# Attention of a hybrid decoder layer: two turns of a loop over head pairs, or one list of 32 items

## The reference

```python
scale = DIFF_HEAD_DIM ** -0.5                       # 64 ** -0.5
logits = einsum('bqhcd,bkhcd->bhcqk', q_blk, k) * scale
logits = logits + bias                              # rel_bias[rel_bucket(dist)]
logits = where(dist >= 0, logits, -inf)
p = softmax(logits, axis=-1)
attn = p[:, :, 0] - lam * p[:, :, 1]                # two maps c = 0, 1 for each head
out = einsum('bhqk,bkhe->bqhe', attn, v)
out = rms_norm(out, subln_g) * (1.0 - lam_init)
```

## Time and profile before

| | |
|---|---|
| median of 3 timed runs | 2877.3 us (2871.14 to 2883.05) |
| the profiled execution | 2897.03 us |
| its span, first to last instruction | 2895.3 us |
| mean granted TensorE clock in it | 0.964 of full |
| `mix`, from its first instruction to its last | about 317 to 502 us of the span |
| its attention loop, turn one and turn two | 325.5 to 406.2, 406.2 to 487.7 us |

### The profile page before, as it was taken

The page is one execution under the profiler, slowest core; times in us unless marked ns, Lnnn a source line. Parts: engine busy times, 40 slices in busy tenths (PEclk is TensorE's granted clock), DMA queues, the critical chain, the costliest instruction groups (busy, mean ns, idle before and its releaser), DMA issues.

```text
span 2895.3 us, 42514 instructions
## 1 busy us (share of the span) xinstructions
PE 2689.3 (93%) x15119; PEld 2367.3 (82%) x15119; DVE 2324.9 (80%) x4258; ACT 1265.2 (44%) x2394; POOL 1077.8 (37%) x779
## 2 busy tenths in 40 slices
PE   7999776979998999999999999988999999999998
PEld 4888544768888999999999999986777777777777
DVE  3562477447889999999899776659999999999998
ACT  4211466222222499999898872222222222222222
POOL 0000000001114444444445665535555555555552
PEclk8999887989999999999999999999999999999999
DMA  6640000314348788989899999989999999999997
GB/s 225 235 169 12 10 0 16 130 73 136 114 133 281 270 313 302 340 301 329 285 330 336 378 379 370 367 303 369 377 389 388 385 384 388 363 387 389 383 376 260
DMA packets 310035, 794.35 MB, mean 274 GB/s; under 512 B 26592, under 2 KB 125568, under 8 KB 305792
## 3 DMA queue, kind: packets, MB, share of 16 engines
q0 software_dynamic: 110592, 402.70, 38.1%
q1 hardware_dynamic: 176832, 301.73, 29.6%
q10 hardware_dynamic: 22464, 88.09, 7.6%
HBM read 694.11 MB, written 98.30 MB: 274 GB/s over the span
## 4 chain that ended last, share of the span: by engine, by line
PE 36%; DVE 17%; DMA 12%; issue 9%; ACT 4%; SPq 1%; DVEq 0%; ACTq 0%
PE ps_up L392 29%; DVE row_sum L119 10%; DMA stage<-v_cols 8%; PE ps_g L439 4%; PE ps_y L802 3%; DMA expert_gate<-g_buf 2%; DMA stage<-expert_act 1%; DVE acc L856 1%; DVE coef_lo L877 1%; ACT key_distance L331 1%; DMA stage<-cols 1%; ACT v_hi L769 1%; DVE fetched L114 1%; ACT second_gate L335 1%; PE ps_g L407 1%
## 5 line engine op out<-in xcount | busy, mean ns | idle before, releaser
L96 POOL DMA_INDIRECT fetched<-u_rows,row_index x384 | 558.3, 1454 | 706.8 <-DVE row_act L114 588.5
L96 POOL DMA_INDIRECT fetched<-v_cols,row_index x384 | 515.4, 1342 | 423.4 <-DVE row_sum L119 367.8
L392 PE MATMUL ps_up<-h_hi,col_hi 128*128 128x320 f32 (+1 forms) x2288 | 555.1, 323 | 38.5 <-DVE col_lo L484 20.0
L392 PE MATMUL ps_up<-h_lo,col_hi 128*128 128x320 f32 (+1 forms) x2288 | 547.3, 320 | 0.0
L392 PE MATMUL ps_up<-h_hi,col_lo 128*128 128x320 f32 (+1 forms) x2288 | 546.7, 319 | 0.0
L114 DVE CUSTOM_DVE_ANT_0 fetched<-fetched,h_rows_then_gates 128x1024 f32<-128x1024 f32 x384 | 452.8, 1222 | 55.5 <-DMA fetched<-u_rows,row_index 42.3
L119 DVE SCALAR_TENSOR_TENSOR row_sum<-fetched,row_act,row_sum 128x1024 f32<-128x1024 f32 x381 | 486.8, 1278 | 1.5 <-DVE row_sum L119 0.5
L802 PE MATMUL ps_y<-v_hi,coef_hi 128*128 128x512 f32 x1280 | 406.0, 399 | 61.6 <-DVE coef_lo L877 57.1
L392 PEld LDWEIGHTS ps_up<-h_hi,col_hi 128*128 128x128 f32 x2288 | 387.8, 190 | 51.0 <-issue 35.2
L769 ACT ACTIVATE v_hi<-stage 128x1024 fp32r<-128x1024 f32 x128 | 135.9, 1062 | 647.9 <-DMA stage<-v_cols 638.1
L802 PE MATMUL ps_y<-v_lo,coef_hi 128*128 128x512 f32 x1280 | 400.6, 395 | 0.0
(11 more groups left out here) (245 smaller groups left out, 3487.3 us busy)
## 6 DMA issues: line engine op xcount, KB each, us to landing
stage<-cols SPq DMA_DIRECT2D x144, 512.0 KB
stage<-v_cols SPq DMA_DIRECT2D x128, 512.0 KB
expert_act<-stage ACTq DMA_DIRECT2D x128, 320.0 KB
expert_gate<-g_buf ACTq DMA_DIRECT2D x20, 2048.0 KB
stage<-expert_act SPq DMA_DIRECT2D x128, 320.0 KB
z_t<-w_ada SPq DMA_DIRECT2D x48, 512.0 KB, 6.1
g_raw<-expert_gate SPq DMA_DIRECT2D x64, 320.0 KB
h_rows_then_gates<-expert_gate SPq DMA_DIRECT2D x64, 320.0 KB
```

The costliest lines, as they stand in the source:

```text
L96: nc.gpsimd.indirect_dma_start(self.buf[:, n % NBUF], None, rows, bass.IndirectOffsetOnAxis(ap=self.at[:, tile, k:k + 1], axis=0)).then_in ...
L392: mm = pe.matmul(ps_up[:, b, half, 0:width], w[:, b, k], h[:, k, a:a + width], start=(k == 0 and i == 0), stop=(k == DC - 1 and i == 2))
```

## The change

The loop over pairs goes. All 32 items (4 heads x 8 query blocks) are one list `ITEMS`, in the order i = 1, 3, 5, 7, 6, 4, 2, 0, each for all four heads, and every engine's list is written out for g = 0 to 31. TensorE's and VectorE's order within an iteration is what it was. ScalarE's becomes far_part(g+2), exps(g+1), copy_t(g), squares(g-2). The scores read q and k directly from slabs 4 to 11 of `z_t`; the scaling by 64 ** -0.5 is given to the ScalarE activations of groups 4 and 5 in `in_project`. The copies at the start of a turn, `far_pair`, `pair_free`, `pair_ready` and the resets of the VectorE step counter are gone; semaphore counts and addresses are constants. Cut to its core:

```diff
@@ in_project, scalar
-                        nc.scalar.activation(z_t[:, m], ps[:, j], ACT.Gelu_apprx_tanh if p < 2 else ACT.Copy).then_inc(copied, 1)
+                        nc.scalar.activation(z_t[:, m], ps[:, j], ACT.Gelu_apprx_tanh if p < 2 else ACT.Copy,
+                                             scale=DH ** -0.5 if p in (4, 5) else 1.0).then_inc(copied, 1)
@@ mix
-        pair_qk = z_t[:, 0:4]
+        q, k = z_t[:, HEADS_A:2 * HEADS_A], z_t[:, 2 * HEADS_A:3 * HEADS_A]
         rising = list(range(1, TT, 2))
-        ORDER = [(a, i) for i in rising + [i - 1 for i in rising[::-1]] for a in range(2)]
-        FAR = [0]
-        for m in range(PAIR):
-            FAR.append(FAR[-1] + (ORDER[m][1] >= 2))
+        ITEMS = [(h, i) for i in rising + [i - 1 for i in rising[::-1]] for h in range(HEADS_A)]
+        N = len(ITEMS)
+        FAR = [sum(i >= 2 for _, i in ITEMS[:g]) for g in range(N + 1)]
@@ mix, scalar
-            with loop(nc, act, 0, HEADS_A // 2) as w:
-                act.wait_ge(pair_free, w + 1)
-                nc.scalar.activation(pair_qk[:, 2:4], z_t[:, bass.ds(8 + 2 * w, 2)], ACT.Copy).then_inc(pair_ready, 1)
-                far_part(w, 0)
-                far_part(w, 1)
-                exps(w, 0)
-                for m in range(PAIR):
-                    if m + 1 < PAIR:
-                        exps(w, m + 1)
-                    if m + 2 < PAIR:
-                        far_part(w, m + 2)
-                    copy_t(w, m)
-                    if m >= 1:
-                        squares(w, m - 1)
-                squares(w, PAIR - 1)
-                act.wait_ge(sq_sum, PAIR * w + PAIR)
+            far_part(0)
+            far_part(1)
+            exps(0)
+            for g in range(N):
+                if g + 2 < N:
+                    far_part(g + 2)
+                if g + 1 < N:
+                    exps(g + 1)
+                copy_t(g)
+                if g >= 2:
+                    squares(g - 2)
+            squares(N - 2)
+            squares(N - 1)
+            act.wait_ge(sq_sum, N)
@@ mix, tensor
-                if m == 0:
-                    pe.wait_ge(pair_ready, 3 * w + 3)
...
-                            mm = pe.matmul(at[:, c, 0:k1 - k0], pair_qk[c * DH:c * DH + DH, hh, i * P:i * P + P],
-                                           pair_qk[c * DH:c * DH + DH, 2 + hh, k0:k1], start=True, stop=True)
+                            mm = pe.matmul(at[:, c, 0:k1 - k0], q[rows, h, i * P:i * P + P], k[rows, h, k0:k1], start=True, stop=True)
...
-            with loop(nc, pe, 0, HEADS_A // 2) as w:
-                pe.wait_ge(pair_free, w + 1)
-                logits(w, 0)
-                logits(w, 1)
-                for m in range(PAIR):
+            logits(0)
+            logits(1)
+            for g in range(N):
@@ mix, vector
-            ch.reset()
-
-            dve.sem_inc(pair_free, 1)
-            with loop(nc, dve, 0, HEADS_A // 2) as w:
-
-                nc.vector.tensor_scalar(pair_qk[:, 0:2], z_t[:, bass.ds(4 + 2 * w, 2)], DH ** -0.5, None, ALU.mult).then_inc(pair_ready, 1)
-                nc.vector.tensor_copy(far_pair[:], far[:, bass.ds(2 * w, 2)]).then_inc(pair_ready, 1)
...
-                output(w, PAIR - 1)
-                dve.wait_ge(o_done, PAIR * w + PAIR)
-                dve.sem_inc(pair_free, 1)
-                ch.reset()
+            for g in range(2):
+                near(g)
+                maximum(g)
+            for g in range(N):
+                combine(g)
+                if g + 2 < N:
+                    near(g + 2)
+                    maximum(g + 2)
+                if g >= 1:
+                    output(g - 1)
+            output(N - 1)
```

More of the change, by code:

```diff
@@ L1574, in far_part @@
[L1574 to L1578, removed]
-                for c in range(2):
[L1580 to L1589, removed]
@@ new lines, in far_part @@
+                if g >= NL:
+                    act.wait_ge(comb_done, g - NL + 1)
+                bias = far[:, h:h + 1]
+                copy = nc.scalar.activation(logit[:, g % NL, :, 0:min(n, HALF)], ps_first[:, :, 0:min(n, HALF)], ACT.Identity, bias=bias)
+                if n > HALF:
+                    act.wait_ge(near_done, g + 1)
+                    copy = nc.scalar.activation(logit[:, g % NL, :, HALF:n], ps_rest[:, :, 0:n - HALF], ACT.Identity, bias=bias)
+                copy.then_inc(far_done, 1)
@@ new lines, in exps, with copy_t @@
+            def exps(g):
+                n = (ITEMS[g][1] + 1) * P
+                act.wait_ge(max_done, g + 1)
+                for c in range(2):
+                    nc.scalar.activation(logit[:, g % NL, c, 0:n], logit[:, g % NL, c, 0:n], ACT.Exp, bias=nmax[:, g % 2, c:c + 1],
+                                         accum_out=ssum[:, g % 2, c:c + 1]).then_inc(exp_done, 1)
+            def copy_t(g):
+                n = ITEMS[g][1] + 1
+                act.wait_ge(t_done, g + 1)
+                if g >= 2:
+                    act.wait_ge(o_mm, g - 1)
+                nc.scalar.activation(att_t[:, g % 2, 0:n], ps_t[:, 0:n], ACT.Copy).then_inc(t_copied, 1)
@@ L1642, in logits, with turn @@
                         if k1 == n:
                             mm.then_inc(l_done, 1)
-            def turn(w, m):
-                pe.wait_ge(comb_done, PAIR * w + m + 1)
-                if m:
-                    pe.wait_ge(t_copied, PAIR * w + m)
-                for j in range(ORDER[m][1] + 1):
-                    mm = pe.transpose(ps_t[:, j], att[:, m % 2, j * P:j * P + P], ident[:])
-                mm.then_inc(t_done, 1)
-            def values(w, m):
-                i = ORDER[m][1]
-                pe.wait_ge(t_copied, PAIR * w + m + 1)
-                if m >= 2:
-                    pe.wait_ge(o_done, PAIR * w + m - 1)
-                col = SW + (2 * w + ORDER[m][0]) * VD
+            def turn(g):
+                pe.wait_ge(comb_done, g + 1)
+                if g:
+                    pe.wait_ge(t_copied, g)
+                for j in range(ITEMS[g][1] + 1):
+                    mm = pe.transpose(ps_t[:, j], att[:, g % 2, j * P:j * P + P], ident[:])
+                mm.then_inc(t_done, 1)
@@ L1659, in values @@
+            def values(g):
+                h, i = ITEMS[g]
+                pe.wait_ge(t_copied, g + 1)
+                if g >= 2:
+                    pe.wait_ge(o_done, g - 1)
+                col = SW + h * VD
                 for j in range(i + 1):
-                    mm = pe.matmul(ps_o[:, m % 2, 0:VD], att_t[:, m % 2, j], z_n[:, j, bass.ds(col, VD)],
-                                   start=(j == 0), stop=(j == i))
+                    mm = pe.matmul(ps_o[:, g % 2, 0:VD], att_t[:, g % 2, j], z_n[:, j, col:col + VD], start=(j == 0), stop=(j == i))
@@ L1675, in _ @@
+            for g in range(N):
+                if g + 2 < N:
+                    logits(g + 2)
+                if g >= 1:
+                    values(g - 1)
+                turn(g)
+            values(N - 1)
             for t in range(TT):
@@ L1746, in _ @@
-            ch.reset()
-            dve.sem_inc(pair_free, 1)
-            with loop(nc, dve, 0, HEADS_A // 2) as w:
-                nc.vector.tensor_scalar(pair_qk[:, 0:2], z_t[:, bass.ds(4 + 2 * w, 2)], DH ** -0.5, None, ALU.mult).then_inc(pair_ready, 1)
-                nc.vector.tensor_copy(far_pair[:], far[:, bass.ds(2 * w, 2)]).then_inc(pair_ready, 1)
-                for m in range(2):
-                    near(w, m)
-                    maximum(w, m)
-                for m in range(PAIR):
-                    combine(w, m)
-                    if m + 2 < PAIR:
-                        near(w, m + 2)
-                        maximum(w, m + 2)
-                    if m >= 1:
-                        output(w, m - 1)
-                output(w, PAIR - 1)
-                dve.wait_ge(o_done, PAIR * w + PAIR)
-                dve.sem_inc(pair_free, 1)
-                ch.reset()
+                if g >= 2:
+                    dve.wait_ge(t_done, g - 1)
```

110 lines of the change are left out of this document (47 added, 63 removed).

## The result

| | before | after |
|---|---|---|
| median of the timed runs | 2876.8 us (4 runs, 2871.1 to 2883.1) | 2838.4 us (4 runs, 2832.6 to 2847.5) |
| ratio | | 0.9869 (0.9835 to 0.9903) |
| profiled execution | 2897.0 us | 2832.6 us |
| `mix`, from its first instruction to the next stage's | 185.4 us | 151.8 us |

The kernel got faster by 38 us, where 28.5 were forecast and 36 was the most that the range allowed. A second timing of the same two kernels gave 0.9864 (0.9841 to 0.9888), 39 us. The direction was right and the circle was there, the size was not right: 33 to 34 us were won in `mix`, and some 5 us more lie outside it.

The account below looks back on a forecast made before the run. The prediction took waits between ScalarE and VectorE in mix as the bound. Gains on VectorE's waits and copies made 31.0 us, less 2.5 for the clock: 28.5 off the median 2877.3, so 2849 us, range 2841 to 2865.

Parts of the forecast that it names:

- VectorE's work on the items is fixed: In mix: VectorE's busy time on items stays (115.7 us without copies), so the gain is read from its waits.
- the deduction for the clock: In mix: dips of TensorE's clock would cost 0 to 6 us in the new order; 2.5 us taken off 31.0.
- the later stages only move forward: Behind mix: engines start anew after the block, so later stages keep their length and only start earlier.
- What binds: In mix: squares waiting for output (39.2 us) and maximum for far copies form one circle between ScalarE and VectorE.
- Late next: In mix after the change: i=7 period 6.1 us, far-copy waits 5.7 us, exps in time by 0.7, TensorE 4.9.
- the single wait: VectorE's maximum at i=7 waiting for the second far copy: 0.82 us for each of four items.
- The sum of 31.0: VectorE's gains in mix: maximum 21.5, addition 5.1, copies 2.8, waits ahead of them 1.4, outputs 1.0, less 0.8.
- The loss of 0.8 at the start: Start of mix at low clock: items i=3 need 3.8 us a period on TensorE against VectorE's 3.4, two periods.
- Off the median whole: The 28.5 us gain, read from mix in the profile, is taken whole off the timed median of 2877.3 us.
- The stall: Rival: ScalarE's far copy stays late in mix; only start and turn are won, gain 10, time 2867; chance 0.13.
- Only the circle goes: Rival: circle cut in mix, but start and turn not won; gain 21.5 less 2.5, 19, time 2858; chance 0.10.
- TensorE as the bound: Slower rival: low clock throughout mix, attention loop 199 us against 162, time 2914; chance 0.03.

Follow-up runs that it names:

- e3: Kernel before, two turns kept, with only ScalarE's order changed to far copies, exps, copy of transposes, squares(m-2): mix 167.2 us, ratio 0.9926.
- e4: Changed kernel with ScalarE's old order back (exps, far copies, copy of transposes, squares(g-1)): mix 171.7 us, ratio 0.9932.
- e8: Changed kernel with the exps ahead of the far copies again, squares(g-2) kept: mix 161.6 us, ratio 0.9887.
- e7: Changed kernel with squares(g-1) in place of squares(g-2), far copies still first: mix 152.4 us, ratio 0.9880.
- e6: Kernel before with its two turns written out, constant addresses and counts, same instruction order: mix 180.7 us, ratio 0.9970.
- e11: Kernel before with two small loads of mix issued in the other order: mix 184.9 us, ratio 0.9992.
- e5: Changed kernel with near(g+2) moved ahead of combine(g) on VectorE for all items: mix 153.7 us, ratio 0.9855.
- e10: Changed kernel with each matmul and transpose of the attention items issued twice: mix 202.2 us, ratio 1.0020 to the kernel before.
- e13: Kernel before with the q scaling factor given to the projection's activations and 1.0 in mix's copy of q: mix 186.0 us, ratio 0.9992.
- e12: Changed kernel with near(g+2) ahead of combine(g) where item g+2 has i=6 or 7, and output scaling moved to ScalarE: mix 138.6 us, ratio 0.9815.

## Why the prediction was right and wrong

The steps that failed are, in the prediction's own terms: "VectorE's work on the items is fixed" (1.9 us), the deduction for the clock (2.5 us) and "the later stages only move forward" (some 5 us). The bullets say what the runs showed in place of each.

- **What binds.** Right. ScalarE's `squares`, VectorE's `output` and what stood behind each were one circle: e3 cut it alone (18.3 us), e4 put it back with the same waits. The reason given for the cut, `squares` moved back by one item, was only half of it: that move alone wins 10.1 of 18.9 us (e8), and the far copies ahead of the exps win all of it without it (e7).
- **Late next.** Right: period 6.00 against 6.1 at i=7, far-copy waits 6.1 us against 5.7, exps in time, TensorE below VectorE. That the single wait came out at 0.82 is in part luck, as its terms were each off by 0.02 to 0.13.
- **The sum of 31.0.** The rows of after give, in its order: maximum's waits 27.2 to 7.0, 20.2 (21.5 forecast); addition 6.1 to 0.5, 5.6 (5.1); copies 2.8 (2.8); waits ahead of them 1.4 (1.4); outputs 2.6 to 0.9, 1.7 (1.0). The loss of 0.8 at the start didn't show: the clock was up at about 329, two items earlier than assumed. Sum 31.7.
- **Missing term.** The step "VectorE's work on the items is fixed, so what leaves is read from its waits" was wrong. Its busy time on the items fell from 115.7 to 113.7 us, as each output starts 0.06 us sooner once its address is a constant. I had seen the register addresses in the code (`bass.ds`) and priced only the copies. This is 1.9 us here; in the old order the loop's form as a whole costs 4.8 (e6). 31.7 and 1.9 are 33.6, what `mix` gained.
- **The clock.** Mis-sized: 2.5 us taken off, with 0 as its bound, and about 0 it was. The clock was 1.00 from 328.7 to 437.9 us, and in the one dip of 3.4 us behind that VectorE didn't wait. Nor could the rows tell how many dips there would be. e11 has the instructions of the kernel before and the same waits of TensorE (up to 1.94 us inside the turns), but outside start, passage and end it has one dip, at 338.2, where the kernel before has four. Its `mix` is 184.9 us against 185.4, so in the old order dips cost nothing either, as the prediction had read. The Trainium skill's case of a TensorE that swings between both levels (TensorE: Matmul & The Clock Gate, A second HAM failure mode: psum-queue depth-cycling) fits the swings of the kernel before, though not the loss of throughput that the page tells of. It doesn't fit the changed one, though TensorE still waits there between its groups, up to 1.4 us. By that rule the gain in `mix` would have been 25, and 33.6 was measured.
- **Off the median whole.** "The later stages only move forward" was wrong. It was argued from the blocks, and is true of the order of work; but timed runs give 38 to 39 us where `mix` gives 33, and the last stage is 4.4 us shorter on average in the profiles with the list. The cause is open, and with it about half of the miss of 10 us; the missing term of 1.9, the clock's 2.5 and the sum's own 0.7 make up the other half.
- **The range.** Its lower end was the sum without its deduction, plus half the spread. It held no allowance for terms left out, so two of them, each small, put the time 2.7 us below it. All unknowns that I had listed could only lower the gain.
- **The rivals.** The stall did not come back elsewhere in the changed kernel; it did in e5, at the scores. "Only the circle goes" had 21.5 us for the circle, and e3 gives 18.3. TensorE as the bound was priced too high, 199 us for the loop against 180 (e10). By its own sum (155 / 96 = 1.6) it would decide from where 60% of TensorE's work runs at the lower level, not 80%.

## What to carry to other kernels

When two engines each wait for the other, follow one item round the circle and ask of each task in it who needs its result and when; put first what the other engine waits for (here the far copies), last what nobody waits for. After that the fullest engine nearly sets the length of the stage, so look at once at what can move from it to an engine with room: cutting the circle and writing the list out gave 33 us, moving one scaling and one addition 14 more. And price a loop's form as well as its contents: in this program an address from a register is an instruction of its own ahead of the one you see.

## What the runs showed of the hardware that was not expected

- An address from a register costs time on the path: 0.05 us ahead of the VectorE output and 0.13 us ahead of the ScalarE `squares` that waits for it (medians over the items). With constants the maximum in turn starts 0.07 us later behind the far copy, so the circle of both engines gets only some 0.12 us shorter, and `mix` 4.8 us with the loop's own branch and passage (e6).
- TensorE's clock held 1.00 from 328.7 to 437.9 us in the changed kernel, with TensorE busy 85.0 of the 105 us shown and waits of up to 1.4 us between its groups. In the kernel before it fell four times outside the starts and the end, with waits of up to 1.95 us; in e11, with the same instructions and waits, once, for 3.4 us (columns as in the earlier trace rows):

```profile
338.30:341.30 3.00, 3.00 (x12) 1.54 (x9) 2.79 (x6) 0.95 (x3) 0.00 (x0) 0.50 0.00 0
```

- A factor other than 1.0 in a ScalarE activation of 128x1024 costs nothing that can be seen: the twelve of the projection take 1024 to 1032 ns in the kernel before, and with the factor in four of them 1024 to 1033 in the changed one and 1023 to 1028 in e13. ScalarE taking an output out of PSUM with a per-row factor was cheap as well: in e12 its instruction of 0.36 us replaced one of 0.35 us on VectorE, and `mix` fell by 9.4.
- The same program reached `mix` at 315.0 and at 317.4 us, and executions of one kernel on one chip differ by 6 to 28 us in time where four or more were timed, while `mix` agreed to 1.0 us between any two profiles of one kernel. A few us in such a stage are read from the profile, not from timed runs.
